# Running the backward scan chunks beside block 0's merge in a Trainium2 trunk-layer kernel

## The chip, the cores and the metric

The kernel runs on one core of one Trainium2 chip. The metric is the device time of one execution in microseconds (us); lower is better. TensorE (PE in the profile), VectorE (DVE), ScalarE (ACT), GpSimd (POOL) and SyncE (SP) each run their own list of instructions in order and meet only at semaphores. 16 DMA engines move the data.

## What is computed

One layer of a hybrid backbone on 128 context tokens (block 0) and 512 latent tokens (blocks 1 to 4), D = 1024, all in float32. Cut to what matters here:

```python
h = rms_norm(x, g_mix_pre) * (1 + sc_a) + sh_a
proj = h @ w_in                     # z, x, B, C, dt, q, k, v, o, gates, merge gates
y = ssd_scan(forward) + flip(ssd_scan(backward)) + D * x      # chunks of 128 tokens
hm = mlstm_scan(forward) + flip(mlstm_scan(backward))
mixed = (gate_ssd * (norm(y * silu(z)) @ w_ssd_out) + gate_ml * (norm(hm) * sigmoid(o) @ w_mlstm_out)) @ w_out
x1 = x + gt_a * rms_norm(mixed)
h2 = rms_norm(x1) * (1 + sc_f) + sh_f
f = peer_ffn(h2)                    # 8 heads, each token fetches its 16 best of 16384 experts (u, v rows)
x2 = x1 + gt_f * rms_norm(f)
```

The scans of the latent tokens run forward through chunks 1 to 4 and backward through 4 to 1. The state that the backward scan hands to chunk b has to be there before chunk b is mixed, so chunks 4, 3 and 2 are first gone through backward for their states alone ("back" chunks).

## The kernel before, in words

Three stages follow each other. `modulate_and_normalise` makes hT, the normalised and turned tokens, [128, 8 k, 640 tokens]. `project_and_scan` multiplies it by most of w_in, with block 0's scan among it. `experts` does all the rest, and holds the change.

`experts` writes one order of work, in `interleave`, which each engine walks through with its own functions. First comes **window 0**: `merge(0, x)` for x = 21 to 61 (block 0's mixers' outputs are normalised, multiplied by w_ssd_out, w_mlstm_out and w_out in twelve pieces of 1 MB each, and turned into h2), and `prepare(0)`. Then the 40 expert heads (8 for each block) follow, 8 steps n for each head m; two heads are chosen ahead (m from -2). The 64 steps that lie beside eight heads are one window, x = 0 to 63: **window 1** runs from head -2 to head 5 and holds what block 1 needs, window 2 the heads 6 to 13 and block 2, and so on. In windows 2 to 4 scan step x is done at x = 0 to 28, and merge step x at 21 to 61.

In a head, PE makes the queries (L1843) and scores (L1851), DVE chooses 16 experts (`choose`, `number_of`), POOL fetches them into the ring's eight slots (L1544, 1 MB each, one slot at a time as slots come free), DVE makes the dot product with u (L1966), ACT makes the coefficient and, for PE, the diagonal (L1671), and the v row is added by PE (L1828) or, for the slots in `ON_VECTOR`, by DVE (L1982): all 32 slots of heads 0 and 1, and every fourth of heads 2 to 5.

Window 1 before is a special one, spaced by `window_one`: x = 4 to 31 hold the 48 steps of the three back chunks, x = 2, 4, ..., 18 nine "late" units (a part of w_in's product, for blocks 1 and 2, that was left over: 16 matmuls of 256 columns, 1 MB of weights), and x = 32 to 63 hold all 29 scan steps and all 41 merge steps of block 1, about three for each x to x = 42. Five more late units stand in window 0, four of them ahead of its matmuls, one at x = 56. The scan, the back chunks and the merge share their tiles (T[0] to T[8], mg, wb) and the banks e_A, e_B and e_spare; so a back chunk can't start before block 0's merge is through (`h2_ready`, 1), and scan 1 not before the back chunks are (`backs_done`). The expert ring holds weights of late units and a result tile at the start, and is free for expert rows early.

A back chunk is a chain over the engines: 8 + 4 transposes (L863, L866), copies on ACT, one multiplication on DVE, the state's 4 matmuls (L915), two steps on DVE (L1100, L1106), 8 transposes of the keys (L927), 4 row matmuls (L933), some ten small steps on DVE, an exponential on ACT, one multiplication (L1156), 8 matmuls of 257 columns on three banks (L984), and after each a step on DVE (L1215).

Of the kernel before, what the change touches and what calls it, by code (L numbers as in the profile page):

```python
# [5 lines left out]
P = 128  # L6
D = 1024
# [44 lines left out]
def semaphores(nc, ctx, prefix=""):  # L52

    taken = []

    def sem(name):
        taken.append(nc.alloc_semaphore(prefix + name))
        return taken[-1]

    def give_back():  # L60
        nc.clear_and_free_semaphores(taken)
        nc.all_engine_barrier()

    ctx.callback(give_back)
    return sem

# [40 lines left out]
def modulate_and_normalise(nc, dr, t, hT, ahead):  # L107
# [3 lines left out]
    with ExitStack() as ctx:  # L111
# [42 lines left out]
        def _(act):  # L154
# [9 lines left out]
            for n in range(2 * BLOCKS):  # L164
                b, half = n // 2, n % 2
                act.wait_ge(turned, n + 1)
                nc.scalar.copy(hT[:, 4 * half:4 * half + 4, b * P:(b + 1) * P], ps[n % 4][:, :, :]).then_inc(moved, 1)
            act.drain()
            act.wait_ge(cols_ready, 1)
            for k in range(3):  # L170
                for c, tokens in enumerate((slice(0, P), slice(P, TOK))):
                    nc.scalar.activation(hT[:, k, tokens], hT[:, k, tokens], ACT.Identity,
                                         scale=cols[:, V_SCALE_A, k, c:c + 1], bias=cols[:, V_SHIFT_A, k, c:c + 1])
# [40 lines left out]
        def _(dve):  # L214
# [34 lines left out]
            for k in range(3, KT):  # L249
                for c, tokens in enumerate((slice(0, P), slice(P, TOK))):  # L250
                    nc.vector.tensor_scalar(hT[:, k, tokens], hT[:, k, tokens], cols[:, V_SCALE_A, k, c:c + 1],
# [122 lines left out]
def project_and_scan(nc, dr, t, hT, ahead):  # L374
# [4 lines left out]
    with ExitStack() as ctx:  # L379
# [139 lines left out]
        def _(pe):  # L519
            pe.wait_ge(par_in, 32)  # L520
            for bank, tokens in ((unit_bank[0], slice(0, 512)), (unit_bank[1][:, 0:P], slice(512, TOK))):
                for k in range(KT):
                    g = SMALL_M * (k % 2)
                    last = nc.tensor.matmul(bank[g:g + SMALL_M, :], ws[:, k, :], hT[:, k, tokens], start=(k < 2), stop=(k >= KT - 2))
# [8 lines left out]
            def channel_tile(n, at, done):  # L533
# [3 lines left out]
                for k in range(KT):  # L537
                    nc.tensor.matmul(pst[m][:, 0:LAT], w[:, j, k, m * P:(m + 1) * P], hT[:, k, P:TOK], start=(k == 0), stop=(k == KT - 1))  # L538
                for k in range(KT):
                    last = nc.tensor.matmul(pst[m][:, LAT:TOK], w[:, j, k, m * P:(m + 1) * P], hT[:, k, 0:P], start=(k == 0), stop=(k == KT - 1))  # L540
# [19 lines left out]
            def unit(k):  # L560
# [9 lines left out]
                if kind == "big":  # L570
                    for k8 in range(KT):
                        last = nc.tensor.matmul(to, hT[:, k8, b * P:(b + 1) * P], w[:, n % W_BUFFERS, k8, :], start=(k8 == 0), stop=(k8 == KT - 1))  # L572
# [145 lines left out]
def scan_steps(nc, dr, t, sem, w, A, B, S, chunks, mstate_banks, preloaded=False, tag="s_", v_written=None):  # L718
# [20 lines left out]
    half = (B[:, 0:512], B[:, 512:1024])  # L739
# [113 lines left out]
    def pe_step(j, s, region_free=None):  # L853
# [50 lines left out]
        if s == 13:  # L904
            pe.wait_ge(B_ready, j + 1)
            pe.wait_ge(xw_ready, j + 1)
            if kind == "sample":
# [3 lines left out]
            for n, d in enumerate(steps):  # L911
                if n:
                    pe.wait_ge(y_read, j + 1)
                for q in range(NG):
                    last = nc.tensor.matmul((B, A)[n][:, q * 256:(q + 1) * 256], Bt[:, q, :], xw[:, where(steps, d), q * 256:(q + 1) * 256],  # L915
                                            start=True, stop=True)
                last.then_inc(state_mm, 1)
        if s == 16:
# [5 lines left out]
            else:  # L924
                pe.wait_ge(xs_ready, j + 1)
# [112 lines left out]
    def dve_step(j, s, region_free=None):  # L1038
# [62 lines left out]
        elif s == 15:  # L1101
            for n, d in enumerate(steps):
                dve.wait_ge(state_mm, H_count(j) + n + 1)
                if prior:
                    dve.drain()
                    nc.vector.tensor_tensor(H[d][:, :], H[d][:, :], (B, A)[n][:, :], ALU.add).then_inc(H_new, 1)  # L1106
                else:
                    nc.vector.tensor_copy(H[d][:, :], (B, A)[n][:, :]).then_inc(H_new, 1)
# [122 lines left out]
    return (sp_step, sp_end, load_x, load_qk), pe_step, act_step, (dve_init, dve_step), (chunk_done, P_mixed, Ks_ready, hm_done, yoff_mm[1], B_turned)  # L1231
# [28 lines left out]
def experts(nc, dr, t, hT):  # L1260

    with ExitStack() as ctx:
# [5 lines left out]
        xb = [sb(f"xb{i}", [P, D]) for i in range(2)]  # L1268
        h2T, qT = sb("h2T", [P, KT, P]), sb("qT", [P, 2, P])
        x1 = [sb(f"x1_{i}", [P, D]) for i in range(2)]  # L1270
# [12 lines left out]
        hT_kept, far_own = sb("hT_kept", [P, KT, 2 * P]), sb("far_w", [P, KT, 2 * P])  # L1283
# [49 lines left out]
        (sp_scan, sp_scan_end, load_x, load_qk), pe_scan, act_scan, (dve_scan_init, dve_scan), (chunk_done, P_mixed, Ks_ready, hm_done, yoff_last, _) = scan_steps(  # L1333
            nc, dr, t, sem, sc, bankA, bankB, bankS[:, :], [("sample", b) for b in range(1, BLOCKS)],
            (bankA[:, 0:512], bankA[:, 512:1024], bankS[:, :]), preloaded=True)
        (sp_back, sp_back_end, _, _), pe_back, act_back, (dve_back_init, dve_back), (backs_done, _, _, _, _, back_x_turned) = scan_steps(
            nc, dr, t, sem, dict(sc, back_keys=T[0][:, :].rearrange("p (m t) -> p m t", t=P)), bankA, bankB, bankS[:, :],
            [("back", b) for b in range(CHUNKS, 1, -1)], (bankA[:, 0:512], bankA[:, 512:1024], bankS[:, :]), preloaded=True, tag="b_")
        pieces_of = lambda ap: ap.rearrange("p (k n) -> p k n", n=256)
        late_w = [pieces_of(expert[:, i, :]) for i in (6, 7, 5, 3, 2)]  # L1340
        late_w += [(mg[:, :, :].rearrange("p q (k n) -> p (q k) n", n=256), pieces_of(m23[:, :]))[i % 2] for i in range(LATE_EARLY, LATE_UNITS)]
        late_to = [acc[:, 0:512], acc[:, 512:1024], bankS[:, :], qs[:, :]]
        late_to += [acc[:, 512 * (u % 2):512 * (u % 2) + 512] for u in range(LATE_FIRST, LATE_UNITS)]
        late_from = [expert[:, 4, 512 * u:512 * u + 512] for u in range(LATE_FIRST)]
        late_from += [T8[:, 512 * (u % 2):512 * (u % 2) + 512] for u in range(LATE_FIRST, LATE_UNITS)]
        late_in, late_mm, late_free, late_out = t["late_in"] + [sem(f"late_in{i}") for i in (2, 3, 4)], sem("late_mm"), sem("late_free"), [sem("late_out0"), sem("late_out1")]
        late_signal = [0, 1] + [2 + (u - 2) % 3 for u in range(2, LATE_UNITS)]
        late_landed = [16, 16] + [16 * ((u - 2) // 3) + 16 for u in range(2, LATE_UNITS)]
        far_w = (far_own, pieces_of(t["held"][:, D:3 * D]))
# [6 lines left out]

        def window_one(at):

            units = [LATE_STEPS[at]] if at in LATE_STEPS else []
            backs = range(max(0, len(BACK_LIST) * (at - 4) // 28), max(0, min(len(BACK_LIST), len(BACK_LIST) * (at - 3) // 28)))  # L1360
            reached = lambda k: 3 * k if k <= 10 else 30 + 2 * (k - 10) if k <= 12 else 34 + 3 * (k - 12) // 2
            steps = range(reached(at - 32), reached(at - 31)) if at >= 32 else range(0)
            return units, [BACK_LIST[i] for i in backs], steps

        def interleave(late, back, scan, merge, far, prepare, body, finish, body_first=False):
# [12 lines left out]

            for x in range(MERGE_FROM, MERGE_TO):
                if x in LATE_AT:  # L1380
                    late(LATE_AT[x])
                merge(0, x)
            for part in range(2):
                prepare(0, part)
            for m in range(-2, HEADS):
                for n in range(GROUPS):
# [4 lines left out]
                    if p == 1:  # L1391
                        units, backs, steps = window_one(at)
                        for u in units:
                            late(u)
                        for j, s in backs:
                            back(j, s)
                        for step in steps:
                            at_step(1, step)
                    elif p < BLOCKS:
# [6 lines left out]
        def _(sp):  # L1406
# [13 lines left out]
            def first_region_free():  # L1420
                sp.wait_ge(late_mm, LATE_UNITS)
                sp.wait_ge(kept, 1)
                load_qk(0)
                sp.wait_ge(backs_done, CHUNKS - 1)
# [777 lines left out]
```

## Time and profile before

| | |
|---|---|
| Runs | 2820.73, 2822.47, 2830.74 us |
| Median | 2822.47 us |
| Profiled execution, its own time | 2825.87 us |
| Its span, from first to last instruction | 2824.1 us |
| Busy: PE, DVE, ACT, POOL | 2402.9, 1626.2, 892.0, 793.7 us |
| Bytes moved | 960.44 MB, 340 GB/s on average |

A row of a timeline gives the start in us from the span's start, the busy us, engine and source line, the operation, the tiles (out<-in) and the count; in brackets stands how long the engine had been idle and what it waited for. A busy PE counts from first to last matmul of a run of them. The trace has two matmul records for each float32 matmul of the program, so that 16 matmuls stand as x32.

### The profile page before, as it was taken

To read this page: it belongs to the slowest core of one execution; us is meant where nothing else is said; L and a number is where in the kernel's file an instruction comes from. 1 tells how busy PE (TensorE), PEld (TensorE's weight loads), DVE (VectorE), ACT (ScalarE), POOL (GpSimd) and SP (SyncE) were. 2 spreads that over 40 slices of the span, in tenths; PEclk is the share of its full clock that TensorE was granted. 3 is DMA by queue.
4 is the path that set the end of the run, shared out by engine and by line. 5 is a ranking of instruction groups with operands and counts; after the bars stand their busy time and mean duration, and the time that the engine had idled before them with its cause. 6 is when DMAs were issued, how large, how long until landed. Compare 5 with 4: busy or idle time off the path is not lost.

```text
span 2824.1 us, 26690 instructions
## 1 busy us (share of the span) xinstructions
PE 2402.9 (85%) x8418; PEld 1348.1 (48%) x8418; DVE 1626.2 (58%) x3765; ACT 892.0 (32%) x2358; POOL 793.7 (28%) x705
## 2 busy tenths in 40 slices
PE   6999999978835787898989899889898998788776
PEld 3555554355733543464666555434464444343332
DVE  2320012211498775798655788656788657666664
ACT  3110111021132332554222455324544324343332
POOL 0111100000132122443222443333333334444453
PEclk8999999989966899999999999999999999999999
DMA  6222325865888699999999999999999999999996
GB/s 253 97 97 97 112 74 226 329 258 216 338 315 333 232 387 422 398 388 410 425 402 424 413 412 383 427 427 426 421 371 411 427 426 426 427 418 427 426 419 284
DMA packets 146591, 960.44 MB, mean 340 GB/s; under 512 B 17250, under 2 KB 28770, under 8 KB 40594
## 3 DMA queue, kind: packets, MB, share of 16 engines
q0 software_dynamic: 96928, 687.39, 59.2%
q1 hardware_dynamic: 36290, 223.12, 20.0%
q10 hardware_dynamic: 13232, 48.24, 4.3%
q8 instruction: 66, 1.08, 0.1%
q14 instruction: 75, 0.61, 0.1%
HBM read 923.50 MB, written 35.19 MB: 339 GB/s over the span
## 4 chain that ended last, share of the span: by engine, by line
PE 29%; DMA 26%; DVE 13%; ACT 4%; DVEq 2%; issue 2%; POOL 1%; ACTq 1%; SPq 0%; POOLq 0%
DMA ring<-in_peer_uv,e_idx 22%; PE e_acc L1828 12%; DVE ring L1966 5%; PE e_spare L1757 3%; PE e_qs L1843 3%; PE e_B L1724 3%; PE e_acc L1742 2%; DMA e_wb<-in_w_out 2%; DVE e_f L1982 2%; PE e_A L1724 2%; DVEq L1968 1%; DMA e_far_w<-in_w_late 1%; ACT e_diag L1671 1%; POOL ring L1544 1%; DMA e_mg<-in_w_late 1%
## 5 line engine op out<-in xcount | busy, mean ns | idle before, releaser
L1828 PE MATMUL e_acc<-ring,e_diag 128*128 128x512 f32 x2256 | 1068.4, 619 | 211.7 <-ACT e_diag L1671 211.6
L1544 POOL DMA_INDIRECT ring<-in_peer_uv,e_idx x640 | 753.5, 1177 | 1479.7 <-PE e_acc L1828 1002.6
L1966 DVE CUSTOM_DVE_ANT_0 ring<-ring,e_xb 128x1024 f32<-128x1024 f32 x640 | 774.1, 1224 | 401.0 <-DMA ring<-in_peer_uv,e_idx 377.8
L1828 PEld LDWEIGHTS e_acc<-ring,e_diag 128*128 128x128 f32 x2256 | 426.7, 197 | 760.9 <-issue 448.2
L1661 ACT ACTIVATE e_act<-e_dots 128x2 f32<-128x2 f32 x320 | 65.0, 203 | 720.8 <-DVEq L1968 715.2
L538 PE MATMUL pj<-held,ring 128*128 128x512 f32 x512 | 225.2, 593 | 0.0
L1671 ACT ACTIVATE e_diag<-ident,e_coef 128x128 f32<-128x128 f32 x564 | 197.9, 394 | 21.2 <-issue 0.3
L572 PE MATMUL pj<-ring,held 128*128 128x512 f32 x352 | 159.8, 610 | 11.1 <-DMA ring<-in_w_big 8.9
L1664 ACT ACTIVATE e_coef<-e_act,e_gate 128x1 f32<-128x1 f32 x640 | 153.8, 287 | 23.3 <-issue 1.3
L1843 PEld LDWEIGHTS e_qs<-e_h2T,e_w_head 128*128 128x128 f32 x1280 | 149.7, 194 | 10.7 <-issue 10.2
L1843 PE MATMUL e_qs<-e_h2T,e_w_head 128*128 128x128 f32 x1280 | 151.0, 277 | 0.8 <-ACT e_h2T L1640 0.8
L1724 PE MATMUL e_B<-e_wb,e_m 128*128 128x512 f32 x320 | 147.5, 607 | 4.6 <-DMA e_wb<-in_w_out 4.6
L538 PEld LDWEIGHTS pj<-held,ring 128*128 128x128 f32 x512 | 94.8, 190 | 107.3 <-issue 107.3
L1982 DVE SCALAR_TENSOR_TENSOR e_f<-ring,e_coef,e_f 128x1024 f32<-128x1024 f32 x74 | 95.1, 1285 | 62.0 <-ACT e_diag L1671 54.9
L572 PEld LDWEIGHTS pj<-ring,held 128*128 128x128 f32 x352 | 67.7, 196 | 93.2 <-issue 90.8
L1724 PEld LDWEIGHTS e_B<-e_wb,e_m 128*128 128x128 f32 x320 | 61.5, 195 | 83.4 <-issue 79.0
L1661 ACT ACT_TABLE_LOAD x76 | 97.5, 1283 | 2.3 <-issue 1.0
L334 DVE COPY ring<-pj 128x160 f32<-128x160 f32 x1 | 0.3, 324 | 143.2 <-PE pj L329 143.2
L1724 PE MATMUL e_A<-e_wb,e_m 128*128 128x512 f32 x160 | 75.1, 615 | 7.2 <-DMA e_wb<-in_w_out 6.7
L984 PE MATMUL e_A<-e_wb,e_m 128*128 128x257 f32 x84 | 28.9, 477 | 51.8 <-DVEq L1157 29.7
L540 PEld LDWEIGHTS pj<-held,ring 128*128 128x128 f32 x512 | 62.2, 192 | 15.3 <-issue 15.3
L513 POOL DMA_DIRECT2D scratch_proj<-tile_out x10 | 6.4, 642 | 217.7 <-ACTq L625 217.7
(403 smaller groups left out, 2453.5 us busy)
## 6 DMA issues: line engine op xcount, KB each, us to landing
e_wb<-in_w_out SPq DMA_DIRECT2D x60, 1024.0 KB, 9.2
e_w_head<-in_w_q ACTq DMA_DIRECT2D x39, 1024.0 KB
ring<-in_w_big SPq DMA_DIRECT2D x18, 2048.0 KB, 8.7
ring<-in_w_mod SPq DMA_DIRECT2D x8, 2048.0 KB, 12.0
ring<-in_peer_uv,e_idx POOLq DMA_INDIRECT x640, 12.4
wm<-in_w_mod SPq DMA_DIRECT2D x4, 2048.0 KB, 18.2
e_m<-scratch_mod_rows SPq DMA_DIRECT2D x15, 512.0 KB, 15.4
e_m<-scratch_xbcT SPq DMA_DIRECT2D x7, 1024.0 KB, 13.4
```

The costliest lines, as they stand in the source:

```text
L538: nc.tensor.matmul(pst[m][:, 0:LAT], w[:, j, k, m * P:(m + 1) * P], hT[:, k, P:TOK], start=(k == 0), stop=(k == KT - 1))
L572: last = nc.tensor.matmul(to, hT[:, k8, b * P:(b + 1) * P], w[:, n % W_BUFFERS, k8, :], start=(k8 == 0), stop=(k8 == KT - 1))
L1544: nc.gpsimd.indirect_dma_start(expert[:, u % RING, :], None, dr["peer_uv"], bass.IndirectOffsetOnAxis(idx[:, h % 4, s:s + 1], 0)).then_inc ...
L1661: nc.scalar.activation(act_v[:, :], dots[:, m % 2, 2 * n:2 * n + 2], ACT.Gelu)
L1664: nc.scalar.mul(coef[:, n % 4, j:j + 1], act_v[:, j:j + 1], gate[:, m % 4, 2 * n + j:2 * n + j + 1])
L1671: last = nc.scalar.mul(diag[:, v % RING, :], t["ident"][:, :], coef[:, n % 4, v - u:v - u + 1])
L1724: last = nc.tensor.matmul(to, src[:, k * P:(k + 1) * P], wb[:, i % 2, k - 4 * part, :], start=(k == 0), stop=(k == KT - 1))
L1757: last = nc.tensor.matmul(bankS[:, 256 * b:256 * (b + 1)], hT_kept[:, k, b * P:(b + 1) * P], far_w[v % 2][:, k, :], start=(k == 0), stop=( ...
L1828: mm = nc.tensor.matmul(acc[:, c * 512:(c + 1) * 512], diag[:, v % RING, :], expert[:, v % RING, D + c * 512:D + (c + 1) * 512], start=Fal ...
L1843: last = nc.tensor.matmul(qs[:, q * P:(q + 1) * P], w_head[:, k, q * P:(q + 1) * P], h2T[:, k, :], start=(k == 0), stop=(k == KT - 1))
L1966: nc.vector.tensor_tensor_reduce(expert[:, u % RING, 0:D], expert[:, u % RING, 0:D], xb[p % 2][:, :], 1.0, 0.0, ALU.mult, ALU.add, dots[:, ...
L1982: nc.vector.scalar_tensor_tensor(f[:, :], value, by, f[:, :], ALU.mult, ALU.add).then_inc(vector_free, 1)
```

## The change

- The back chunks get tiles and banks of their own, in slots 0 to 4 of the expert ring and in e_acc, e_qs and e_spare, and their 48 steps are spread over x = 21 to 61 of window 0, about 1.2 for each x, each behind the merge's own step. `scan_steps` takes `narrow` for this: with it the state's matmuls write A (e_acc), and the row matmuls a bank of 512 (e_qs).
- Six late units now stand in window 0, at x = 21, 22, 25, 27, 29 and 31, each with its result at x + 1, in the banks e_A and e_B, which the merge needs from x = 32. Their weights come through ring slots 6, 7 and 5: SP loads unit u + 3 after unit u's matmuls, and does so ahead of its merge step of that x. Eight more stand in window 1, at x = 0, 2, 3, 5, 6, 8, 9 and 11, with weights in a tile of their own and in that of x1/xb of odd blocks.
- Window 1 is laid as the later ones: scan step x at x = 0 to 28, merge step x at 21 to 61. The loads for scan 1 come at x = 50 of window 0 and x = 12 of window 1.
- GpSimd starts fetching experts when the back chunks are done and stored.
- hT is laid [128, 5 blocks, 8 k, 128], so that a matmul that streams 512 tokens reads four runs of 128 elements. The copy of hT for later units (`hT_kept`) is made by ACT at the start of `experts`.

```diff
-LATE_UNITS, LATE_FIRST, LATE_EARLY = len(LATE), 4, 5
-LATE_AT = {24: 0, 25: 1, 26: 2, 27: 3, 56: 4}
-LATE_STEPS = {2 * (u - LATE_EARLY) + 2: u for u in range(LATE_EARLY, LATE_UNITS)}
-LATE_RESULT_STEP = 2 * (LATE_UNITS - LATE_EARLY) + 2
+LATE_UNITS, LATE_EARLY = len(LATE), 6
+LATE_AT = {21: 0, 22: 1, 25: 2, 27: 3, 29: 4, 31: 5}
+LATE_STEPS = {0: 6, 2: 7, 3: 8, 5: 9, 6: 10, 8: 11, 9: 12, 11: 13}
+LATE_OVER = 12
...
-                    nc.tensor.matmul(pst[m][:, 0:LAT], w[:, j, k, m * P:(m + 1) * P], hT[:, k, P:TOK], start=(k == 0), stop=(k == KT - 1))
+                    nc.tensor.matmul(by_block(pst[m][:, 0:LAT]), w[:, j, k, m * P:(m + 1) * P], hT[:, 1:BLOCKS, k, :], start=(k == 0), stop=(k == KT - 1))
...
-    half = (B[:, 0:512], B[:, 512:1024])
+    half = (B[:, 0:512], B[:, 512:1024]) if narrow is None else (None, narrow)
+    state_to = B if narrow is None else A
...
+            backs_of = lambda x: len(BACK_LIST) * (x - MERGE_FROM) // (MERGE_TO - MERGE_FROM)
             for x in range(MERGE_FROM, MERGE_TO):
+                if x - 1 in LATE_AT:
+                    late(LATE_AT[x - 1], True)
                 if x in LATE_AT:
-                    late(LATE_AT[x])
+                    late(LATE_AT[x], False)
                 merge(0, x)
+                for j, s in BACK_LIST[backs_of(x):backs_of(x + 1)]:
+                    back(j, s)
...
-                    if p == 1:
-                        units, backs, steps = window_one(at)
...
-                    elif p < BLOCKS:
+                    if p < BLOCKS:
+                        if p == 1 and x - 1 in LATE_STEPS:
+                            late(LATE_STEPS[x - 1], True)
+                        if p == 1 and x in LATE_STEPS:
+                            late(LATE_STEPS[x], False)
+                        if p == 1 and x == LATE_OVER:
+                            late(None, False)
                         at_step(p, x)
...
+            def late(u, result):                      # SP
+                if result:
+                    return
+                if u is None:
+                    sp.wait_ge(late_mm, LATE_UNITS)
+                    load_qk(0)
+                elif u < 3:
+                    sp.wait_ge(late_mm, u + 1)
+                    late_load(u + 3)
                 elif u > LATE_EARLY and u + 1 < LATE_UNITS:
                     sp.wait_ge(late_mm, u)
                     late_load(u + 1)
...
                     if p == 0:
-                        for u in range(2, LATE_EARLY):
-                            late_load(u)
+                        late_load(2)
...
             pool.wait_ge(late_mm, LATE_EARLY)
+            pool.wait_ge(back_H_out, 16 * (CHUNKS - 1))
+            pool.wait_ge(back_C_out, 32 * (CHUNKS - 1))
+            pool.wait_ge(backs_done, CHUNKS - 1)
...
                 if x == 32:                           # PE
                     pe.wait_ge(scaled, p + 1)
+                    if not p:
+                        pe.wait_ge(late_free, LATE_EARLY)
```

## Rows read from the trace of the kernel before

**Rows 1.** The page's 40 slices of 70.6 us: granted PE clock and DMA share, in tenths.

```profile
PEclk8999999989966899999999999999999999999999
DMA  6222325865888699999999999999999999999996
```

**Rows 2.** By stage: length; PE, PEld, DVE, ACT, POOL busy us; clock; DMA share; GB/s.

```profile
574.00:679.00 105.00, 88.42 (x288) 54.91 (x288) 16.52 (x27) 20.70 (x36) 0.00 (x0) 0.92 0.62 234
679.00:750.00 71.00, 66.99 (x347) 59.37 (x348) 23.89 (x80) 11.04 (x19) 7.62 (x8) 0.95 0.79 302
750.00:889.00 139.00, 56.52 (x245) 45.84 (x244) 111.53 (x204) 31.52 (x73) 43.42 (x30) 0.65 0.85 321
889.00:1156.00 267.00, 208.80 (x720) 121.10 (x718) 190.56 (x430) 94.28 (x243) 66.33 (x62) 0.88 0.89 355
...
1603.00:1696.00 93.00, 86.06 (x354) 51.99 (x355) 76.83 (x187) 51.29 (x138) 40.48 (x34) 1.00 1.01 414
1696.00:1797.00 101.00, 87.12 (x320) 49.76 (x318) 81.45 (x214) 49.18 (x127) 37.59 (x32) 0.98 0.96 396
...
1797.00:1999.00 202.00, 180.20 (x528) 87.28 (x528) 126.50 (x297) 68.27 (x192) 72.73 (x64) 0.97 1.01 427
```

**Rows 3.** Timelines of POOL and DVE: first fetch, first dots of heads 0, 2, 6.

```profile
730.31 1.03 POOL L1544 DMA_INDIRECT ring<-in_peer_uv,e_idx  x1 [170.69 <-DVEq L2052]
...
749.82 1.23 DVE L1966 CUSTOM_DVE_ANT_0 ring<-ring,e_xb 128x1024 f32<-128x1024 f32 x1 [0.17 <-issue]
...
888.85 1.23 DVE L1966 CUSTOM_DVE_ANT_0 ring<-ring,e_xb 128x1024 f32<-128x1024 f32 x1 [0.24 <-issue]
...
1156.28 1.23 DVE L1966 CUSTOM_DVE_ANT_0 ring<-ring,e_xb 128x1024 f32<-128x1024 f32 x1 [0.18 <-issue]
```

**Rows 4.** Timelines of SP, ACT and PE over window 0's beginning.

```profile
573.85 0.34 SPq L1528 DMA_DIRECT2D e_w_head<-in_w_q  x1
...
584.11 1.06 ACT L1590 ACTIVATE e_m<-e_m 128x1024 f32<-128x1024 f32 x1 [25.34 <-DMA e_m<-scratch_proj]
...
574.81 16.54 PE L1742 MATMUL e_acc<-ring,held 128*128 128x256 f32 x64 [11.37 <-DVE e_zero L2095]
591.18 7.07 PE L1742 MATMUL e_spare<-ring,held 128*128 128x256 f32 x32
...
607.35 7.13 PE L1724 MATMUL e_A<-e_wb,e_m 128*128 128x512 f32 x16 [0.44 <-DVE e_m L1909]
```

**Rows 5.** Timelines of ACT and PE over window 0's end.

```profile
665.27 1.02 ACT L1623 ACTIVATE e_sq<-e_B 128x1024 bf16<-128x1024 f32 x1 [16.51 <-PE e_B L1724]
...
666.47 1.28 ACT L1628 ACT_TABLE_LOAD   x1
...
679.08 5.31 PE L1843 MATMUL e_qs<-e_h2T,e_w_head 128*128 128x128 f32 x32 [0.77 <-ACT e_h2T L1640]
```

**Rows 6.** Timeline of PE in window 1: steps of back chunks and late units.

```profile
699.24 1.07 PE L863 MATMUL e_A<-ident,e_m 128*128 128x128 f32 x8 [0.59 <-DMA e_m<-scratch_xbcT]
...
707.49 1.89 PE L915 MATMUL e_B<-e_m,e_wb 128*128 128x256 f32 x8
...
732.95 1.03 PE L984 MATMUL e_A<-e_wb,e_m 128*128 128x257 f32 x4
...
763.15 9.33 PE L1742 MATMUL e_acc<-e_mg,held 128*128 128x256 f32 x32 [8.36 <-DMA e_mg<-in_w_late]
...
794.67 2.08 PE L984 MATMUL e_A<-e_wb,e_m 128*128 128x257 f32 x4 [9.49 <-DVEq L1157]
```

**Rows 7.** The chain of work that ended last: start, us, what.

```profile
745.37 17.74 DMA e_mg<-in_w_late
```

**Rows 8.** Costliest groups of PE from 1603 to 1696 us, of DVE from 750 to 889.

```profile
L1828 PE MATMUL e_acc<-ring,e_diag 128*128 128x512 f32 x134 | 60.4, 596 | 7.0 <-ACT e_diag L1671 7.0
...
L1982 DVE SCALAR_TENSOR_TENSOR e_f<-ring,e_coef,e_f 128x1024 f32<-128x1024 f32 x29 | 37.3, 1285 | 3.5 <-issue 0.4
```

**Rows 9.** The page's groups: the matmuls that stream 512 latent tokens of hT.

```profile
L538 PE MATMUL pj<-held,ring 128*128 128x512 f32 x512 | 225.2, 593 | 0.0
```

More of the change, by code:

```diff
@@ L166, in _ @@
                 act.wait_ge(turned, n + 1)
-                nc.scalar.copy(hT[:, 4 * half:4 * half + 4, b * P:(b + 1) * P], ps[n % 4][:, :, :]).then_inc(moved, 1)
+                nc.scalar.copy(hT[:, b, 4 * half:4 * half + 4, :], ps[n % 4][:, :, :]).then_inc(moved, 1)
             act.drain()
@@ L520, in _ @@
             pe.wait_ge(par_in, 32)
[L521 removed]
+            for bank, blocks in ((unit_bank[0], slice(0, 4)), (unit_bank[1][:, 0:P], slice(4, BLOCKS))):
                 for k in range(KT):
                     g = SMALL_M * (k % 2)
[L524 removed]
+                    last = nc.tensor.matmul(by_block(bank[g:g + SMALL_M, :]), ws[:, k, :], hT[:, blocks, k, :], start=(k < 2), stop=(k >= KT - 2))
                 last.then_inc(small_parts, 1)
@@ L571, in unit @@
                     for k8 in range(KT):
-                        last = nc.tensor.matmul(to, hT[:, k8, b * P:(b + 1) * P], w[:, n % W_BUFFERS, k8, :], start=(k8 == 0), stop=(k8 == KT - 1))
+                        last = nc.tensor.matmul(to, hT[:, b, k8, :], w[:, n % W_BUFFERS, k8, :], start=(k8 == 0), stop=(k8 == KT - 1))
                 else:
@@ L906, in pe_step @@
             pe.wait_ge(xw_ready, j + 1)
+            if narrow is not None:
+                pe.wait_ge(xs_ready, j + 1)
             if kind == "sample":
@@ L914, in pe_step @@
                 for q in range(NG):
-                    last = nc.tensor.matmul((B, A)[n][:, q * 256:(q + 1) * 256], Bt[:, q, :], xw[:, where(steps, d), q * 256:(q + 1) * 256],
+                    last = nc.tensor.matmul((state_to, A)[n][:, q * 256:(q + 1) * 256], Bt[:, q, :], xw[:, where(steps, d), q * 256:(q + 1) * 256],
                                             start=True, stop=True)
@@ new lines, in experts @@
+        assert cut[-1] <= 5 * 2 * D
+        (sp_back, sp_back_end, _, _), pe_back, act_back, (dve_back_init, dve_back), (backs_done, _, _, _, _, back_H_out, back_C_out) = scan_steps(
+            nc, dr, t, sem, dict(sc, **bk), acc, None, bankS[:, :],
+            [("back", b) for b in range(CHUNKS, 1, -1)], (acc[:, 0:512], acc[:, 512:1024], bankS[:, :]), preloaded=True, tag="b_", narrow=qs[:, :])
+        pieces_of = lambda ap: ap.rearrange("p (k n) -> p k n", n=256)
+        second_w = x1b[:, :, :].rearrange("p i (k n) -> p (i k) n", n=256)
@@ L1350, in experts @@
+        late_landed = [16, 16, 16, 32, 32, 32] + [16 * ((u - LATE_EARLY) // 2) + 16 for u in range(LATE_EARLY, LATE_UNITS)]
+        far_w = (w_own, pieces_of(t["held"][:, D:3 * D]))
         far_from = [xb[KEPT_BLOCK % 2][:, 512 * i:512 * i + 512] for i in range(2)]
@@ L1494, in merge @@
                     piece(p, PIECE_AT.index(x) + 2)
+                elif x == 45 and p == 0:
+                    late_load(LATE_EARLY)
+                    for j in range(2):
+                        sp.wait_ge(late_out[j], 16 * LATE_EARLY // 2)
+                    late_load(LATE_EARLY + 1)
                 if x == 36:
@@ L1610, in merge @@
                     last.then_inc(scaled, 1)
-                elif x == 33 and p == 0:
-                    for u in range(LATE_FIRST):
-                        late_result(u)
                 elif x == 36:
@@ L1756, in far @@
                     for k in range(KT):
-                        last = nc.tensor.matmul(bankS[:, 256 * b:256 * (b + 1)], hT_kept[:, k, b * P:(b + 1) * P], far_w[v % 2][:, k, :],
+                        last = nc.tensor.matmul(bankS[:, 256 * b:256 * (b + 1)], hT_kept[:, b, k, :], far_w[v % 2][:, k, :],
                                                 start=(k == 0), stop=(k == KT - 1))
```

145 lines of the change are left out of this document (62 added, 83 removed).

## The prediction, made before the changed kernel was run

> **What bounds the kernel now.** I read the page's slices first: from about 1000 us on the 16 DMA engines are at 0.9 to full share to the end, and only ahead of that is there room [rows 1]. The table by stage says the same: 0.62, 0.79, 0.85 and 0.89 share from 574 to 1156 us, then 0.96 to 1.01 [rows 2]. So the last 1700 us run at the pace at which expert rows come in, and the kernel ends earlier only if head 6, with which window 2 begins, begins earlier. That date is what I forecast: head 6's first dot, 1156.3 us now [rows 3]. From there on the order of work, its bytes and its state are the same in both kernels.
>
> Up to it there are four stretches. Window 0, 574 to 679: PE is busy for 88 of 105 us [rows 2], four late units, twelve pieces, one late unit. The head of window 1, 679.1 [rows 5] to the first dot at 749.8 [rows 3]: PE busy for 67 of 71 [rows 2]. Heads 0 and 1, to 888.9 [rows 3]: DVE busy for 111.5 of 139 us, PE for 56.5 at a mean granted clock of 0.65 [rows 2], so nearer to 1.2 than to 2.4 GHz: DVE makes dots and products, the back chunks come beside them, and nobody waits for PE's rate. Heads 2 to 5, to 1156.3: 267.4 us at 0.89 DMA share, with scan 1 and merge 1 pressed together; the same four-head stretch of window 3, with the merge alone, takes 202 us at 427 GB/s [rows 2].
>
> **Window 0, its beginning.** Now four late units in a row take 574.8 to 605.0, the first two 16.5 us because the clock is low at first, the others 6.9 (two starts, 591.2 and, by the same length, 598.1) [rows 4]; the pieces begin at 607.4 [rows 4]. What takes long from here is order, not work. SP now waits for late unit 0 (done at 574.8 + 16.5 - 6.9 = 584.4) ahead of all its loads: z, y, hm, then the back chunk's x. The nearest row for such a queue is ACT's wait: the branch tiles landed at 584.1, 10.3 us after SP's first issue, with some 3.2 MB ahead or among them [rows 4]. The first back x has 3.5 MB before and with it (a late weight, three branch tiles, itself), so 11 us: 595.5. PE's back transposes stand ahead of late unit 1 in its order, so that PE is idle from 584.4 to 595.5. Then 1.7 us of transposes [rows 6], or double after idleness, and late unit 1 in 9.3 us, by the unit that ran after 8.4 us of idleness [rows 6]: 608. SP issues z-gate loads, o and late unit 2's weights only behind unit 1: 3.5 MB again, 11 us: 619, unit 2 to 628 (9.3). Key transposes and row matmuls 2 us, units 3, 4, 5 at 6.9 each: 651. The last result must leave e_A and e_B before the merge's transposes: 0.6. First state matmuls 1.4, transposes 2, the other five state matmuls with their DVE answers 4 (a DVE step of 257 columns is about 0.5): the pieces begin at 659, **51 later than now**. Bounds: added PE work alone, two units and two thirds of a back chunk, 14 + 7 = 21; and 65, if each of the two weight loads takes the longest queue seen, 17.7 us for late weights that fell in with other loads [rows 7], 7 more for each of two.
>
> **The pieces.** Now 607.4 to 665.3, 58 us [rows 4, 5], with PE 42 us in pieces and most of the rest waiting for weights. Chunk 4's end, chunk 3 whole and half of chunk 2 come in: a chunk is 1.7 + 1.9 + 2.0 + 8 x 0.51 = 9.7 us of PE [rows 6], so 13 us here. The waits for weights hide some, but v for chunk 3 is only asked for one step before its use, behind a 1 MB piece (4 to 5 us of idle PE), and late weights for window 1 (2 MB), back states and back inputs (4 MB) share the DMA engines. I take 70: **+12**, bounds 0 and +25. **The end.** 665.3 to 679.1 now [rows 5], a chain ACT, DVE, ACT, DVE, PE. Ten back steps stand in it, each behind a step of the chain on the same engine: exponential and square root take turns on ACT, so two more table loads of 1.28 [rows 5], 1.3 for each of two big DVE steps, three rounds of state matmuls. **+8**, bounds +4 and +15. Window 1 begins at 679 + 51 + 12 + 8 = 750.
>
> **Window 1 to the first dot.** Now 70.7. Ahead of x = 16 there stand eight late units, 55.3 us, and scan steps 0 to 15 with two heads' queries: window 3's same stretch has PE at 86.1 with 60.4 of expert products among it [rows 2, 8], so 26. With the queries of head 2, and some waits for weights (the load of unit u + 1 is issued behind unit u - 1, so it has a unit's 6.9 us beside PE's other steps and mostly fits), the first dot comes after 92: **+21**. Bounds: 85 and 105. Fetching begins some 20 us ahead of it, 824 against 730.3 [rows 3].
>
> **Heads 0 and 1.** DVE's work: 81.5 in window 3's like stretch, less 4 for a block's end, plus 32 products of 1.285 [rows 2, 8] = 118, against 111.5 now. With the idle share of now a little smaller, since its back chunks made DVE wait for PE, **138, so -1**. Bounds 125 and 150. **Heads 2 to 5.** 202 in place of 267.4: **-65**, bounds 192 and 212. DVE has 16 products more than in window 3, PE fewer, and both fit beside the transfers.
>
> **The sum.** 51 + 12 + 8 + 21 - 1 - 65 = +26 us at head 6, and at the end. On the profiled execution 2825.9 + 26 = 2852; that execution lies 3.4 above the median, so 2849 is my time. At 980 us (750 + 92 + 138) the changed kernel stands at head 2's first dot with scan 1 behind it; the one before is a head further then, with scan 1 still in work.
>
> Costed at nothing: the strided stream of hT, as 512 columns cost 593 ns in one record with no idle time [rows 9] and four runs of 128 are the same columns; were each record 1% longer it would be 2 to 3 us. ACT's early copy of hT (2 us) lies in its 10 us wait for the branches [rows 4]. SP's moved scan loads (x at x = 50, q and k at 12) land before their use. GpSimd's new waits are over by head 0's choice.
>
> A rule against this change: PE that waits between short bursts works at the lower clock; the row shows it, a unit of 9.33 in place of 6.9 after 8.4 us idle, and 2.08 for 1.03 after 9.5 [rows 6]. The Trainium skill, "TensorE: Matmul & The Clock Gate", section HAM oscillation, says that repeated waits for DMA make each next stretch begin cold. By the rows I have counted this twice at the beginning; by that page it would come back at every wait among the pieces too, which is the third rival.
>
> **The rivals.**
> 1. Faster. The back chunks do hide: loads land in 6 or 7 us, PE fills its waits, and window 0 grows by added PE work only, 7 for a unit and 3 x 9.7 = 29, so 36 with nothing for the chain; heads 0 and 1 lose half of DVE's 27 us idle, -9. 36 + 21 - 9 - 65 = -17: 2806. The 17 us of PE idle in window 0 [rows 2] speak for it, SP's order against it.
> 2. No change. Window 0 grows by 55 in place of 71, and heads 2 to 5 run in 192, since DMA had more room before them: 55 + 21 - 1 - 75 = 0: 2822. The point from which faster and slower part is 45 us of growth in window 0, with the other terms as I have them.
> 3. Much slower. PE stays near 1.2 GHz over window 0: late units 1 to 5 take 9.3 or more (+7 beyond mine), twelve pieces 3.5 us longer each where nothing hides it; half of that, 21, and the back chunks' matmuls 10 longer: +38, so +64: 2887.
> 4. It does not do what it says: back steps end late and GpSimd's first fetch waits for their stores instead of the choice. That would show as fetches later than head 0's choice; by the order it can't last more than some us. It adds 5 to mine.
>
> **Chances.** My forecast with rival 4: 0.52; rival 1: 0.15; rival 2: 0.2; rival 3: 0.13. A measurement here tells 0.5%, 14 us, from no change. Mine reaches from +8 to +45 and so gives a little to "same", rival 1 as well. Faster 0.13, same 0.27, slower 0.60. Range: 2808 to 2885, which leaves out the far half of rivals 1 and 3.
>
> **What would show it.** Right: the first matmul of the pieces near 659, window 1's first query matmul near 750, the first fetch near 824, dots of heads 0, 2, 6 near 842, 980, 1182, DMA share near 0.6 to 0.7 until 840, and back steps between late units on PE with an idle stretch of 10 us on each side of unit 1. Wrong: pieces that begin before 640 (the loads land sooner than by the nearest row), a pieces stretch over 85 us (lockstep costs more), or heads 2 to 5 that don't come down to 202, in which case the pressing together of scan and merge was not what held them.

## The result, and the profile after

The changed kernel takes 2832.74 us (median of 6 runs), the kernel before 2822.94 us: a ratio of 1.0032, with a 95% interval of 1.0020 to 1.0045. It is slower by some 9 us. The forecast was 26 us slower, so the direction was right and the size nearly three times too large. The profiled execution took 2832.3 us, with a span of 2830.6 us; the profiled execution of the kernel before took 2825.87 us.

The table by stage of the changed kernel: stretch, its length, then busy us of PE, PE's weight loads, DVE, ACT, POOL (counts), clock, DMA share, GB/s.

```profile
574.00:656.00 82.00, 58.32 (x261) 50.25 (x262) 15.04 (x30) 20.44 (x32) 0.00 (x0) 0.84 0.60 226
656.00:750.00 94.00, 67.61 (x216) 38.13 (x216) 30.68 (x52) 13.76 (x20) 0.00 (x0) 0.91 0.64 233
750.00:842.00 92.00, 87.42 (x490) 78.75 (x489) 33.92 (x104) 19.63 (x50) 7.63 (x8) 0.96 0.63 223
842.00:968.00 126.00, 42.22 (x195) 36.17 (x194) 115.41 (x241) 34.76 (x91) 41.53 (x30) 0.61 0.84 318
968.00:1167.00 199.00, 156.00 (x445) 74.18 (x443) 148.74 (x315) 64.65 (x179) 68.59 (x64) 0.93 1.01 426
```

Set beside [rows 2], window 0 is 71 us longer (574 to 750 against 574 to 679), the stretch to the first dot 21 longer, heads 0 and 1 are 13 shorter, heads 2 to 5 68 shorter and now at full DMA share. The dates of the first fetch and of the first dots of heads 0, 2 and 6, from the timelines of POOL and DVE, answer to [rows 3]:

```profile
823.84 1.04 POOL L1564 DMA_INDIRECT ring<-in_peer_uv,e_idx  x1 [265.20 <-DVEq L2065]
...
842.17 1.23 DVE L1979 CUSTOM_DVE_ANT_0 ring<-ring,e_xb 128x1024 f32<-128x1024 f32 x1 [0.16 <-issue]
...
967.84 1.23 DVE L1979 CUSTOM_DVE_ANT_0 ring<-ring,e_xb 128x1024 f32<-128x1024 f32 x1 [0.18 <-issue]
...
1167.03 1.23 DVE L1979 CUSTOM_DVE_ANT_0 ring<-ring,e_xb 128x1024 f32<-128x1024 f32 x1 [0.18 <-ACT e_diag L1682]
```

Head 6 begins at 1167.0 in place of 1156.3, 10.7 us later; the span ends 6.5 us later, the medians lie 9.8 apart. What PE does at the beginning of window 0 (its timeline) answers to [rows 4]: late unit 0, a wait for the back chunk's x, late unit 1, a wait for late unit 2's weights, and the pieces from 655.8 on.

```profile
575.19 9.11 PE L1752 MATMUL e_A<-ring,held 128*128 128x256 f32 x32 [12.74 <-DVE e_zero L2108]
596.57 1.97 PE L869 MATMUL e_acc<-ident,ring 128*128 128x128 f32 x8 [12.27 <-DMA ring<-scratch_xbcT]
...
599.18 7.29 PE L1752 MATMUL e_A<-ring,held 128*128 128x256 f32 x32
606.31 1.89 PE L923 MATMUL e_acc<-ring 128*128 128x256 f32 x8
618.42 9.67 PE L1752 MATMUL e_B<-ring,held 128*128 128x256 f32 x32 [10.22 <-DMA ring<-in_w_late]
...
655.76 4.56 PE L1733 MATMUL e_A<-e_wb,e_m 128*128 128x512 f32 x10
```

### The profile page after: what moved, and what is told of

Same layout as the page of the kernel before. It is cut to its first block, busy times and chain, and to the rows that moved or that the text cites. A ratio compares the mean times of both kernels' runs of the same rounds, so it can differ in the third digit from the quotient of the medians.

```text
span 2830.6 us, 26686 instructions
## 1 busy us (share of the span) xinstructions
PE 2395.8 (85%) x8418; PEld 1344.9 (48%) x8418; DVE 1627.2 (57%) x3765; ACT 885.6 (31%) x2352; POOL 790.2 (28%) x705
## 4 chain that ended last, share of the span: by engine, by line
PE 29%; DMA 28%; DVE 13%; ACT 3%; DVEq 2%; issue 2%; POOL 2%; ACTq 1%; SPq 0%; POOLq 0%
DMA ring<-in_peer_uv,e_idx 24%; PE e_acc L1842 12%; DVE ring L1979 5%; PE e_spare L1767 3%; PE e_qs L1857 3%; PE e_acc L1752 2%; PE e_B L1733 2%; PE e_A L1733 2%; DVE e_f L1995 2%; POOL ring L1564 2%; DMA e_far_w<-in_w_late 1%; DVEq L1981 1%; ACT e_diag L1682 1%; PE e_A L1752 1%; DMA e_wb<-in_w_out 1%
## 5 line engine op out<-in xcount | busy, mean ns | idle before, releaser
L1979 DVE CUSTOM_DVE_ANT_0 ring<-ring,e_xb 128x1024 f32<-128x1024 f32 x384 | 465.3, 1225 | 246.0 <-DMA ring<-in_peer_uv,e_idx 232.6
L1979 DVE CUSTOM_DVE_ANT_0 ring<-ring,e_x1b 128x1024 f32<-128x1024 f32 x256 | 309.7, 1224 | 168.0 <-DMA ring<-in_peer_uv,e_idx 157.8
L1995 DVE SCALAR_TENSOR_TENSOR e_f<-ring,e_coef,e_f 128x1024 f32<-128x1024 f32 x74 | 95.1, 1285 | 41.9 <-ACT e_diag L1682 34.8
## 6 DMA issues: line engine op xcount, KB each, us to landing
ring<-in_w_mod SPq DMA_DIRECT2D x8, 2048.0 KB, 12.3
```

The source lines that it names most:

```text
L1979: nc.vector.tensor_tensor_reduce(expert[:, u % RING, 0:D], expert[:, u % RING, 0:D], xb[p % 2][:, :], 1.0, 0.0, ALU.mult, ALU.add, dots[:, ...
L1995: nc.vector.scalar_tensor_tensor(f[:, :], value, by, f[:, :], ALU.mult, ALU.add).then_inc(vector_free, 1)
```

## The experiments

Each was timed against the kernel before on the same chip. Ratios are to that kernel; the changed kernel's is 1.0032. A difference of two ratios is uncertain by about 0.002 to 0.004. Dates come from each run's own trace, which is one execution, and such a date can be off by 5 us: the kernel before with nothing but another layout of hT, whose time can't be told from its own, has head 6's first dot here (DVE's timeline), against 1156.28 in [rows 3]:

```profile
1151.44 1.22 DVE L1970 CUSTOM_DVE_ANT_0 ring<-ring,e_xb 128x1024 f32<-128x1024 f32 x1 [0.18 <-issue]
```

### SP's order at the beginning of window 0

```diff
             def late(u, result):                      # SP, changed kernel
                 if result:
+                    if u < 3:
+                        sp.wait_ge(late_mm, u + 1)
+                        late_load(u + 3)
                     return
...
-                elif u < 3:
-                    sp.wait_ge(late_mm, u + 1)
-                    late_load(u + 3)
```

> The changed kernel with one thing moved on SP: in window 0 the wait for late unit u (0, 1, 2) and the load of unit u + 3 come one merge step later, so the branch tiles, the back chunk's inputs and late unit 2's weights are issued at once, and unit 0 is waited for only behind them. My theory (window 0's beginning is long by the order of SP's issues, two stretches of 12.3 and 10.2 us in which PE waits for a load): both waits go, PE begins the pieces near 633 us in place of 655.8, window 1 near 728 in place of 750, and the time falls by 18 to 23 us, to about 2812. Rival (the DMA engines are shared, so the loads land as late as before, or the chain of the back chunk on ACT and DVE takes the place of the waits): the pieces begin at 648 or later and the time falls by less than 8.

Measured: 2820.69 us, ratio 1.0002 (0.9991 to 1.0013). PE's timeline in this kernel, with the date of head 6 from DVE's:

```profile
585.72 1.09 PE L869 MATMUL e_acc<-ident,ring 128*128 128x128 f32 x8 [1.62 <-DMA ring<-scratch_xbcT]
...
601.28 9.72 PE L1752 MATMUL e_B<-ring,held 128*128 128x256 f32 x32 [5.40 <-DMA ring<-in_w_late]
...
638.68 1.55 PE L1733 MATMUL e_A<-e_wb,e_m 128*128 128x512 f32 x3
...
1154.88 1.22 DVE L1979 CUSTOM_DVE_ANT_0 ring<-ring,e_xb 128x1024 f32<-128x1024 f32 x1 [0.18 <-issue]
```

The first wait fell from 12.3 to 1.6 us, the second only from 10.2 to 5.4. The pieces begin 17 us earlier, head 6 at 1154.9 (12 earlier), and the ratio is 0.0030 lower, 8.5 us, with some 5 us of uncertainty either way. So the order was a cost of its own, about as large as the whole loss, though smaller than the 18 to 23 us expected.

One reason is that the edit does less than was expected of it. The wait for unit 0 now stands at the head of x = 22, and the load of late unit 2's weights is in merge step 22, so it is still issued behind that wait and behind unit 3's weights, o and the gates. SP's timeline has it as the first of these two:

```profile
585.46 9.06 SPq L1452 DMA_DIRECT2D ring<-in_w_late  x2
```

The weights landed at 601.3, 15.8 us after their issue. Beyond that, 5 of the 17 us won at the pieces are gone by head 6, which no run explains.

### The layout of hT alone

```diff
-        hT = t["held"][:, 0:KT * TOK].rearrange("p (k t) -> p k t", t=TOK)
+        hT = t["held"][:, 0:KT * TOK].rearrange("p (b k t) -> p b k t", k=KT, t=P)
```

with every use of it, on the kernel before.

> The kernel before with only the layout of hT changed to [128, 5 blocks, 8 k, 128], as in the change: matmuls that stream 512 tokens read four runs of 128. My theory: nothing, 2823 within 2 us, and 593 ns for each of the 512-column records. Rival (the strided stream costs PE time in the first two stages): each record 1 to 2% longer, 2826 to 2831, which would be up to all of the 9.8 us by which the changed kernel is slower.

Measured: 2822.85 us, ratio 1.0006 (0.9995 to 1.0017). The group of 512-column matmuls between 100 and 574 us:

```profile
L543 PE MATMUL pj<-held,ring 128*128 128x512 f32 x425 | 186.9, 593 | 0.0
```

Four runs of 128 elements cost the same 593 ns as one of 512 [rows 9]. No part of the result can be put down to the layout.

### A third weight buffer in the kernel before

```diff
-        late_w += [(mg[...], pieces_of(m23[:, :]))[i % 2] for i in range(LATE_EARLY, LATE_UNITS)]
+        late_w += [(mg[...], pieces_of(m23[:, :]), far_own[:, :, :])[(i - LATE_EARLY) % 3] for i in range(LATE_EARLY, LATE_UNITS)]
...
                 if u == LATE_EARLY:                   # SP
                     region_free(1)
                     late_load(u)
                     late_load(u + 1)
+                    late_load(u + 2)
-                elif u > LATE_EARLY and u + 1 < LATE_UNITS:
+                elif u > LATE_EARLY and u + 2 < LATE_UNITS:
                     sp.wait_ge(late_mm, u)
-                    late_load(u + 1)
+                    late_load(u + 2)
```

> The kernel before with a third buffer for the weights of late units 5 to 13 (the tile that is idle until block 2), so each is loaded one unit earlier. Theory 1 (DVE's idle time in heads 0 and 1 was one wait of 16.0 us behind PE, which waited for a late unit's weights; that is why these heads fell from 139 to 125.6 us with the change, where I had forecast 138): the wait shrinks below 6 us, heads 0 and 1 take 126 to 130 us, and the time falls by 8 to 14, to about 2811. Theory 2 (the idle time belongs to the back chunks' chain over PE, ACT and DVE at the low clock, spread over their steps): heads 0 and 1 stay above 135 and the time within 3 us.

Measured: 2806.07 us, ratio 0.9945 (0.9924 to 0.9966). In the kernel before, DVE's timeline in head 0 has this row, the one long wait of heads 0 and 1:

```profile
777.86 0.69 DVE L1125 TENSOR_REDUCE e_s_emax<-e_B 128x4 f32<-128x512 f32 x1 [15.96 <-PE e_B L933]
```

and with the third buffer the same step and the table by stage show:

```profile
764.42 0.69 DVE L1125 TENSOR_REDUCE e_s_emax<-e_B 128x4 f32<-128x512 f32 x1 [5.18 <-PE e_B L933]
```

```profile
747.00:875.00 128.00, 54.14 (x244) 44.51 (x242) 111.40 (x204) 31.52 (x73) 43.27 (x30) 0.66 0.89 341
```

Heads 0 and 1 take 128 us in place of 139 with the same 111.4 us of DVE work and the back chunks still among them. The stretch lost 10.8 us, and this one wait fell by 10.8 us. So the larger part of the idle time, 16 of 27 us, was one wait, through PE's order behind a late unit whose weights were under way (the 8.4 us row of [rows 6]), and not a share that goes with the work. Theory 1 holds. The third buffer as a whole was worth 0.0055 of the time, some 15 us, with 6 us of uncertainty either way; it also loads the other late units' weights earlier.

### The back chunks left out, in their old place and in their new one

On the kernel before and on the changed kernel the 48 back steps and their waits were taken out, and scans 1 to 3 load the given state:

```diff
-                sp.dma_start(H[1][:, :], dr["state_ssd"][1] if b == CHUNKS else dr["back_ssd"][b]).then_inc(H_in, 16)
+                sp.dma_start(H[1][:, :], dr["state_ssd"][1]).then_inc(H_in, 16)
```

> The kernel before with the three back chunks left out (the backward scan of every block starts from the given state, so block 1 to 3's results are not the reference's). It prices them where they were, in window 1. Theory: heads 0 and 1 lose 18 us of DVE work and most of the 16 us wait, 139 to about 106 us, the stretch ahead of them a few us; the time falls by 33 to 42, to about 2785. Rival (in window 1 they were hidden beside late units and transfers, which is why moving them brought nothing): it falls by less than 20.

> The changed kernel with the three back chunks left out (every backward scan starts from the given state, so blocks 1 to 3 are not the reference's). It prices them in their new place, as the run before priced them in window 1 (40 us). Theory, by the trace of the changed kernel: without them PE's 12.3 us wait for the back chunk's x goes, the weights of late unit 2 come sooner, the pieces begin near 630 (655.8 with them), take 58 us again (73.6 with them) and the end 14 us (20.6 with them), so window 1 begins near 702 in place of 750 and the time falls by 45 to 50, to about 2785. That they cost more in window 0 than in window 1 is the reason for the missing gain. Rival (they are cheap in window 0, and what costs is the two late units more and SP's order): it falls by less than 30.

Measured: 2780.04 us, ratio 0.9854 (0.9827 to 0.9882) without them before; 2796.18 us, ratio 0.9922 (0.9901 to 0.9943) without them after the change. So they cost 0.0146, some 41 us, in window 1, as expected (33 to 42), and 1.0032 - 0.9922 = 0.0110, some 31 us, in window 0. The two prices differ by 0.0036, and that difference is itself uncertain by 0.0037. Head 6's dates point the same way. Timelines of DVE, first without the back chunks before the change, then after it:

```profile
1113.03 1.22 DVE L1963 CUSTOM_DVE_ANT_0 ring<-ring,e_xb 128x1024 f32<-128x1024 f32 x1 [0.18 <-issue]
```

```profile
1132.23 1.23 DVE L1971 CUSTOM_DVE_ANT_0 ring<-ring,e_xb 128x1024 f32<-128x1024 f32 x1 [0.18 <-issue]
```

1156.3 - 1113.0 = 43.3 before, 1167.0 - 1132.2 = 34.8 after: by these dates moving the chunks gained 8.5 us. With four dates of single executions in it that gain is likely but not shown. What remains is 1132.2 - 1113.0 = 19.2 us for the rest of the change (the late units, SP's order, the new layout of window 1), and 19.2 - 8.5 is the 10.7 us found. The rest's loss is resolved in the times too: 0.9922 - 0.9854 = 0.0068, 19 us, with 10 us of uncertainty either way. My theory for the second run, 45 to 50 us, missed: without back chunks PE waits 14.7 us for late unit 2's weights, longer than with them, so that the pieces begin at 640.7 and not at 630:

```profile
607.30 16.39 PE L1746 MATMUL e_B<-ring,held 128*128 128x256 f32 x64 [14.71 <-DMA ring<-in_w_late]
```

### The late units of window 1 cut to an eighth

```diff
+                some = KT if u < LATE_EARLY else 1
                 for b in range(2):
-                    for k in range(KT):
+                    for k in range(some):
```

on both kernels, with `stop` at the last of them; weights, waits and results stay.

> The changed kernel with the late units 6 to 13 of window 1 cut to 2 of their 16 matmuls each (the product of the first 128 of 1024 inputs, so blocks 1 and 2 are not the reference's); weights, waits and results stay. It prices their matmuls, 8 x 6.1 = 48 us of PE, in the stretch ahead of head 0, of which PE is busy for 87 of 92 us. Theory (that stretch is bound by PE, and a stretch ahead of head 6 counts in full): the first dot comes 25 to 40 us earlier, the loads of weights being the next bound, and the time falls by as much. Rival (the loads or scan 1's chain are nearly as long): under 12.

> The kernel before with the same cut, units 5 to 13, 9 x 6.1 = 54 us of PE, in window 1 at x = 2 to 18. Theory: here they stand beside back chunks and the wait for weights, so the first dot comes 10 to 20 us earlier and heads 0 and 1 lose some of the 16 us wait; the time falls by 15 to 30, less than in the changed kernel: packing the units ahead of x = 12 is then what the rest of the change costs. Rival: as much as or more than in the changed kernel, and then the cost of the rest lies in window 0 alone.

Measured: ratio 0.9926 (0.9906 to 0.9946) on the changed kernel, 0.9919 (0.9899 to 0.9939) on the one before. The stage ahead of head 0, first in the changed kernel, then in the one before (679 to 731), by the tables by stage (the first row reaches 5 us into head 0, which starts at 809.8):

```profile
750.00:815.00 65.00, 47.39 (x300) 43.11 (x301) 40.21 (x121) 21.83 (x55) 7.70 (x8) 0.87 0.90 341
```

```profile
679.00:731.00 52.00, 31.67 (x164) 27.16 (x164) 23.38 (x79) 11.04 (x19) 7.63 (x8) 0.81 0.93 366
```

In the changed kernel the first dot came 32.4 us earlier (809.8) and heads 0 and 1 kept their 125.6; the time fell by 0.0106, 30 us, for eight units. In the kernel before it came 18.3 earlier (731.5) and heads 0 and 1 lost 6; the time fell by 23 us for nine units. Both are as expected. At the first dot the units' matmuls gave back 32 of 48 us where they are packed ahead of x = 12, and 18 of 54 us where they are spaced over x = 2 to 18; at head 6 it is 32 (1135.0) and 24 us (1132.3). So they were hidden better in their old places, and in the new ones PE is nearly the bound. By the times alone, 0.0106 against 0.0081, the difference isn't resolved.

### Products of heads 0 and 1 on PE

With no late unit left in e_acc from x = 12 on, PE can take expert products from head 0 on:

```diff
-ON_VECTOR = [u < 2 * TOPK or u < 6 * TOPK and u % 4 == 0 ...
+ON_VECTOR = [u < 6 * TOPK and u % 4 == 0 ...
-FIRST_ON_PE = 2
+FIRST_ON_PE = 0
```

> The changed kernel with e_acc used for expert products from head 0 on: of the 32 slots of heads 0 and 1 every fourth stays with DVE, the other 24 go to PE, which the change makes possible since no late unit is left in e_acc then. Theory (heads 0 and 1 are bound by DVE, 115 of 126 us busy, with PE idle for two thirds): DVE loses 24 x 1.285 = 31 us, the stretch falls from 125.6 to about 97 (85 us of DVE, some 38 MB to fetch), the time by 24 to 30. Rival (the longer way dots, ACT's diagonal, PE, slot free, at PE's low clock, holds the eight slots back): the stretch stays above 115 and the time falls by less than 12.

> SP's order of the first run and PE's products from head 0 together, on the changed kernel. If a stretch ahead of head 6 is worth its own length at the end, the two add: 12 by the first, 24 to 30 by the second, so 2792 or a little less. Rival (one uses up the other, since DMA is then the bound from head 0 on): the sum falls short by 8 or more.

> The kernel before with the third buffer of the third run (2806) and head 1's slots on PE but for every fourth; head 0 must stay with DVE there, since late units fill e_acc to x = 18. Theory (DVE bounds head 1 too): 12 x 1.285 = 15 us less of DVE work, time 9 to 14 below 2806, about 2795. Rival (in window 1 before the back chunks' chain binds head 1, not DVE): within 4 of 2806. The comparison with the run above says which of the two arrangements is the better base once both are mended.

Measured: 2815.20 us, ratio 0.9983 (0.9971 to 0.9994) for the first; 2794.76 us, 0.9921 (0.9903 to 0.9939) with SP's order; 2798.40 us, 0.9936 (0.9915 to 0.9957) for head 1 on PE in the kernel before with the third buffer. Heads 0 and 1 of the first, by its table by stage:

```profile
848.00:947.00 99.00, 76.46 (x271) 45.42 (x270) 86.77 (x217) 43.31 (x115) 31.21 (x30) 0.90 0.97 391
```

DVE had 115.4 us of work in 126 and has 86.8 in 99: the stretch shortens by 26 us, nearly as the work does, and the DMA share comes to 0.97. Of that, 0.0049, 14 us, is seen in the time: heads 2 to 5 take 203 in place of 199, and in this execution the pieces took 3 us more and their beginning 2. My 24 to 30 were too much. Together with SP's order the ratio falls by 0.0111, more than the 0.0079 of the two alone, within what the intervals allow, so there is no sign that one uses up the other. Head 1 in the kernel before gave 0.0009, unresolved in time, where 9 to 14 us were expected, though the trace has head 1 at 54 us in place of 65 and head 6 at 1126.8 in place of 1142.4; that trace is of the fastest of its four executions, the one it is set beside of the slowest. Mended in these ways, the changed arrangement (0.9921) and the one before (0.9936) can't be told apart.

### Weights first, and back steps out of the end

```diff
-                    if p == 0:                        # SP, x = 22
-                        late_load(2)
...
                     if not p:                         # SP, x = 21
+                        late_load(2)
                         sp.dma_start(T[0][:, :], dr["y_ssd"][0]).then_inc(branches_in, 16)
...
-            backs_of = lambda x: len(BACK_LIST) * (x - MERGE_FROM) // (MERGE_TO - MERGE_FROM)
+            backs_of = lambda x: min(len(BACK_LIST), len(BACK_LIST) * (x - MERGE_FROM) // (MERGE_TO - 6 - MERGE_FROM))
```

Both start from the kernel with SP's order and products of heads 0 and 1 on PE (0.9921). The first hunk is the first run, both are the second.

> The kernel of the two changes together (SP's order, PE's products from head 0), and late unit 2's weights as SP's first load of window 0. With the order alone PE still waited 5.4 us for them and ran the unit in 9.7 in place of 6.9 us. Theory: both go, the pieces begin near 631 in place of 638.8, and the time falls by 5 to 8 us below that kernel's, a ratio of about 0.990 to the kernel before. Rival (the branch tiles or the back chunk's x are now late by as much): no change.

> The kernel above, with the back steps spread over x = 21 to 55 of window 0 in place of 61, so that none stands in the chain at its end. Theory: the end, 20.6 us with ten back steps in it and 13.9 before, falls back by 5 to 7 us, and the pieces lengthen by 2 to 4, so 2 to 4 us of time are gained. Rival (the steps cost the same anywhere, or the pieces' stretch pays more because its transfers compete): none, or a loss to 5 us.

Measured: 2793.19 us, 0.9905 (0.9887 to 0.9922), and 2792.66 us, 0.9898 (0.9881 to 0.9914). Against 0.9921 neither step is resolved. In the trace of the first the wait for late unit 2's weights is gone and the pieces begin at 632.8 in place of 638.8, as expected, but PE then waits 8.9 us in place of 6.4 for chunk 3's v, and head 6 is only 2 us earlier. In the trace of the second, the way from the last piece to h2 is 13.4 us in place of 17.0, and the pieces begin 10 us later after late unit 0 than in the first: what the end gave, the beginning took. Both kernels are about 1% faster than the kernel before and 1.3% faster than the changed one.

## Why the prediction was right and wrong

**Window 0, its beginning: right.** 51 longer forecast, 48 measured (655.8 against 607.4), by the steps named: the pause behind unit 0 ends with the landing of the back chunk's x at 596.6 (forecast 595.5), unit 2 starts at 618.4 (619). The first experiment shows that SP's order made at least 17 of the 48; late unit 2's weights waited for unit 0 there too.

**The pieces and the end: right.** 655.8 to 729.4 is 74 us, forecast 70; PE does wait for chunk 3's v, 6.5 us. The matmuls of the pieces and of the back states, from 656 to 730 us:

```profile
L1733 PE MATMUL e_B<-e_wb,e_m 128*128 128x512 f32 x64 | 29.1, 599 | 5.6 <-DMA e_wb<-in_w_out 5.5
...
L992 PE MATMUL e_acc<-ring 128*128 128x257 f32 x12 | 4.4, 504 | 6.5 <-DMA ring<-scratch_proj 6.5
```

The end took 20.6 us to the next late unit, forecast 22. Late unit 6 begins at 750.0, where I had window 1 begin. The two table loads are there: ACT loads tables at 732.1, 733.6 and 737.7 where it had loaded one [rows 5].

**The stretch to the first dot: right.** 842.2 - 750.0 = 92.2, forecast 92; first fetch 823.8, forecast 824. PE busy for 87.4 of 92.

**Heads 0 and 1: wrong, the term that failed.** Forecast 138, -1; measured 125.6, -13. I took DVE's work nearly right (118 forecast, 115.4 found), and then added 20 us of idle time as a share of the stretch, where 10 were found, "with the idle share of now a little smaller". The idle time of that stretch before was not a share: 16.0 of its 27 us were one wait, behind a late unit whose weights were late, and the change removes it, as no late unit and no back chunk is left in the stretch. DVE's waits of that stretch, listed one by one, have it in the first line. The third-buffer run showed the cause: it took 10.8 us of that wait away and left DVE's work and the back chunks, and the stretch fell by 10.8, to 128. (In rival 1, half of the 27 us idle off and 7 us of work on would be -7 and not -9, and its sum -15.)

**Heads 2 to 5:** 199 against 202 forecast, at full DMA share. No run moves the scan and merge steps alone, but all the traces agree: with window 1 spread as the later ones this stretch takes 199 to 204 us, with scan 1 and merge 1 pressed together 264 to 268, whatever else was changed. **The sum:** 48 + 16 + 7 + 21 - 13 - 68 = 11 at head 6. Of the 15 us by which my 26 was too large, 12 are heads 0 and 1, 3 heads 2 to 5; the smaller misses of window 0 cancel.

**From head 6 to the end** I took no difference. The profiled executions give back 4 us of the 10.7, the medians 1. In the other traces head 6's shift and the span's agree within 6 us: -13.9 and -17.5 for the third buffer, -43.3 and -43.6 without back chunks, -29.3 and -33.8 for order and products together.

**The rivals.** Rival 1 had the mended wait in it ("heads 0 and 1 lose half of DVE's 27 us idle") but with window 0 growing by 36; the truth had window 0 by my forecast and heads 0 and 1 nearer to rival 1's. Rival 2, no change, came near to the time but not by its terms: window 0 grew by 71 us and not by 55, and heads 2 to 5 took 199 and not 192. Rival 3, PE at the low clock over window 0, did not come: the granted clock was 0.84 and 0.91 in its two parts, late units 3 to 5 took their full-clock length (7.07 us, and 13.98 for two), and a record among the pieces took 599 ns against 626 before. The 626 come of the kernel before's own short waits. PE's timeline shows one, and the sixteen records behind it, which take 7.1 us elsewhere:

```profile
647.48 0.66 PE L1791 MATMUL e_A<-ident,e_m 128*128 128x128 f32 x4 [2.59 <-DVE e_m L1923]
647.97 8.73 PE L1724 MATMUL e_B<-e_wb,e_m 128*128 128x512 f32 x16
```

What the Trainium skill says against the change (TensorE: Matmul & The Clock Gate, HAM oscillation) held where I counted it, a unit of 9.67 us after 10.2 us idle, and at the wait for chunk 3's v, after which the four records of a back state took 2.05 us in place of 1.03, but not at each wait among the pieces: after waits of 0.6 to 2.1 us their eight records took 3.7 us each time. Rival 4 can't be seen: the fetch waited for the choice, with the back chunks through.

**What the change was for.** The pressing together of scan 1 and merge 1 did go, 68 us, and the whole of it was spent before: 48 + 23 in window 0 and 21 in the packed late units, against 13 for heads 0 and 1. By the runs without back chunks, moving them reads as a gain of 8.5 us at head 6, which is not resolved; all the rest of the change, the packing of late units and SP's waits ahead of its loads before all, is a loss of 19, which is.

## What to carry to other kernels

Before idle time is carried over to a new plan as a share, ask which waits it consists of: here one wait, behind another engine's order and one transfer, was 16 of 27 us, and a third buffer for such transfers gave 0.55%. A wait put ahead of a list of loads on an issuing queue delays all of them, and can cost the engine that needs the first of them its landing time: here PE stood still for 12.3 and 10.2 us. Work that is moved into a stretch where its engine is nearly the bound costs more than in a place where it was partly hidden: here 32 of 48 us against 24 of 54.

## What the runs showed of the hardware that was not expected

The price of a pause to PE was nearly the same for pauses of 5 to 15 us. A late unit takes 7.07 us where none stands before it, and 13.98 for two. It took 9.72 us after 5.4 us idle, 9.33 after 8.4, and 9.67 after 10.2, and two units took 16.39 after 14.7: 2.3 to 2.7 us more each time. Behind 12.3 us of idleness the short transposes took most of it over (1.97 in place of 1.04 us for the eight, 1.06 in place of 0.60 for the four), and the unit that followed them took 7.29.
